# One weight block for both token halves, in two banks by turns, in the gate and z projections of a hybrid decoder layer

## The reference, cut to what matters

```python
hn = rms_norm(x, norm_mix)
proj = einsum('bsd,dn->bsn', hn, w_in) + b_in
z_att = proj[..., OFF_Z_ATT:OFF_GATES]                       # 512 channels
gates = sigmoid(proj[..., OFF_GATES:].reshape(b, s, 2, 1024)) # 2048 channels
...
att = sum(softmax(lse over groups) * out of each group)       # 512 channels
y_att = att * silu(z_att)
merged = gates[:, :, 0] * (y_rnn @ w_o_rnn) + gates[:, :, 1] * (y_att @ w_o_att)
x = x + merged @ w_out
x = x + sigmoid(rms_norm(x) @ w_ple_gate + b) * (p @ w_ple)
```

## Time and profile before

| what | value |
|---|---|
| median of 3 runs | 1347.05 us (1346.85 to 1347.11) |
| the profiled execution, its time | 1346.43 us |
| its span, first to last instruction | 1344.6 us |
| PE busy | 1330.4 us, 99% |
| DVE, ACT, POOL busy | 788.4, 506.8, 535.5 us |

### The profile page before, as it was taken

The page is one execution under the profiler, slowest core; times in us unless marked ns, Lnnn a source line. Parts: engine busy times, 40 slices in busy tenths (PEclk is TensorE's granted clock), DMA queues, the critical chain, the costliest instruction groups (busy, mean ns, idle before and its releaser), DMA issues.

```text
span 1344.6 us, 17628 instructions
## 1 busy us (share of the span) xinstructions
PE 1330.4 (99%) x6254; PEld 1103.4 (82%) x6254; DVE 788.4 (59%) x1257; ACT 506.8 (38%) x1281; POOL 535.5 (40%) x500
## 2 busy tenths in 40 slices
PE   8999999999999999999999999999999999999998
PEld 6887888888888888888888888888888788888887
DVE  6799888842779666565665752159612466234323
ACT  7455646542434444344443688311200011223100
POOL 6975424404458334041340632353166317044020
PEclk9999999999999999999999999999999999999999
DMA  6232312332202032120320332376379545122111
GB/s 239 79 102 87 104 61 79 110 100 71 75 13 83 25 90 66 29 83 24 95 59 29 114 102 85 99 244 211 102 280 414 178 129 154 58 79 63 40 48 47
DMA packets 84470, 139.50 MB, mean 104 GB/s; under 512 B 10048, under 2 KB 41120, under 8 KB 84384
## 3 DMA queue, kind: packets, MB, share of 16 engines
q10 hardware_dynamic: 39936, 75.82, 15.9%
q1 hardware_dynamic: 44448, 62.56, 15.7%
HBM read 108.84 MB, written 29.51 MB: 103 GB/s over the span
## 4 chain that ended last, share of the span: by engine, by line
PE 86%; DVE 5%; DMA 5%; ACT 2%; issue 1%; POOL 0%; SPq 0%; ACTq 0%; POOLq 0%; DVEq 0%
PE bank L1257 26%; PE bank L1262 26%; PE bank L1261 26%; DMA g_in<-gate_dram 4%; PE bank L1407 2%; PE bank L1387 2%; PE bank L1374 1%; PE bank L1396 1%; DVE xc L991 1%; PE bank L1500 1%; DMA x_nat<-in_x 0%; ACT L736 0%; DVE ibuf L1018 0%; PE bank L1300 0%; DVE qkr L1099 0%
## 5 line engine op out<-in xcount | busy, mean ns | idle before, releaser
L539 POOL TENSOR_TENSOR ring<-raw,ring 128x512 fp32r<-128x512 f32 x221 | 311.8, 1411 | 724.7 <-PE bank L1262 642.3
L1257 PE MATMUL bank<-hn,ring 128*128 128x512 f32 x640 | 251.8, 393 | 2.3 <-DVE sgbuf L979 1.2
L1262 PE MATMUL bank<-hn,ring 128*128 128x512 f32 x640 | 249.4, 390 | 0.0
L1261 PE MATMUL bank<-hn,ring 128*128 128x512 f32 x640 | 249.2, 389 | 0.0
L1257 PE MATMUL bank<-ring,hn 128*128 128x512 f32 x576 | 232.6, 404 | 0.2 <-POOL ring L539 0.2
L1262 PE MATMUL bank<-ring,hn 128*128 128x512 f32 x576 | 225.8, 392 | 0.0
L1261 PE MATMUL bank<-ring,hn 128*128 128x512 f32 x576 | 225.2, 391 | 0.0
L543 POOL TENSOR_SCALAR ring<-raw 128x512 fp32r<-128x512 f32 x221 | 186.6, 844 | 8.2 <-DMA raw<-in_w_rnn_s 8.1
L1257 PEld LDWEIGHTS bank<-hn,ring 128*128 128x128 f32 x640 | 120.2, 188 | 27.4 <-DVE sgbuf L979 1.6
L1262 PEld LDWEIGHTS bank<-hn,ring 128*128 128x128 f32 x640 | 120.1, 188 | 25.4
L1261 PEld LDWEIGHTS bank<-hn,ring 128*128 128x128 f32 x640 | 120.2, 188 | 23.9
(11 more groups left out here) (181 smaller groups left out, 2157.4 us busy)
## 6 DMA issues: line engine op xcount, KB each, us to landing
raw<-in_w_tail_s SPq DMA_DIRECT2D x104, 256.0 KB, 2.7
g_in<-gate_dram ACTq DMA_DIRECT2D x48, 256.0 KB, 3.1
raw<-in_w_rnn_s SPq DMA_DIRECT2D x45, 256.0 KB, 2.7
raw<-in_w_qkv_s SPq DMA_DIRECT2D x48, 192.0 KB, 2.5
gate_dram<-g_out ACTq DMA_DIRECT2D x32, 256.0 KB, 2.1
raw<-in_w_qkv_s SPq DMA_DIRECT2D x48, 128.0 KB, 2.2
o_dram<-o_buf ACTq DMA_DIRECT2D x48, 128.0 KB, 1.8
o_in<-o_dram ACTq DMA_DIRECT2D x12, 512.0 KB, 3.7
```

The lines of the kernel that those rows point to most:

```text
L539: nc.gpsimd.tensor_tensor(ring[:, ring_slot(p), 1], raw[:, p % RAW], ring[:, ring_slot(p), 0].bitcast(F32), ALU.subtract).then_inc(w_ready, 1)
L1257: ins = T.matmul(out, lhs[0], rhs[0], start=first, stop=False)
L1261: T.matmul(out, lhs[0], rhs[1], start=False, stop=False)
L1262: return T.matmul(out, lhs[1], rhs[0], start=False, stop=last)
```

## The change

Slots 2m and 2m + 1 are taken together as a pair. For each block of weights TensorE runs six matmuls: high by high for half 0 and half 1, high by low for both, low by high for both. So successive products alternate between two banks, and both banks are complete at the end of the pair. TensorE waits for both banks at the pair's start. The order list puts both slots of a pair at the pair's end; attention steps stay after the same number of products.

```diff
-        if K % KD == 0:
-            order.append(("slot", K // KD - 1))
+        slot = K // KD - 1
+        if K % KD == 0 and slot < SLOTS_Q:
+            order.append(("slot", slot))
+        elif K % (2 * KD) == 0 and slot >= SLOTS_Q:
+            order += [("slot", slot - 1), ("slot", slot)]
         if K in STEP_AT:
             order.append(("step", STEP_AT[K]))
...
+            def both_halves(n, first_block, blocks, rhs_of, after_block):
+
+                for b in range(blocks):
+                    p, c = divmod(first_block + b, 4)
+                    need(p)
+                    w_hi, w_lo = part(p, slice(c * P, (c + 1) * P))
+                    x_hi, x_lo = zip(*(rhs_of(h)(b) for h in range(2)))
+                    for i, (w, x) in enumerate(((w_hi, x_hi), (w_hi, x_lo), (w_lo, x_hi))):
+                        for h in range(2):
+                            ins = T.matmul(bank[(n + h) % 4][:], w, x[h], start=b == 0 and i == 0,
+                                           stop=b == blocks - 1 and i == 2)
+                            if used[0]:
+                                ins.then_inc(w_used, used[0])
+                                used[0] = 0
+                            if b == blocks - 1 and i == 2:
+                                ins.then_inc(proj_done, 1)
+                    if c == 3:
+                        used[0] = 1
+                    after_block(b)
 
             for q, (kind, t, h) in enumerate(Z_MAIN):
                 n = N_Z + q
                 bank_free(n)
-                transposed(n, 4 * FIRST_TAIL + (q // 2) * KD, KD, perm_half(h), h == 1, step_after(q))
+                if h == 0:
+                    bank_free(n + 1)
+
+                    def steps_after(b):
+                        for K in (KD * (SLOTS_Q + q) + 2 * b + 1, KD * (SLOTS_Q + q) + 2 * b + 2):
+                            if K in STEP_AT:
+                                attention(STEP_AT[K])
+
+                    both_halves(n, 4 * FIRST_TAIL + (q // 2) * KD, KD, perm_half, steps_after)
```

## The result

| | before | with the change |
|---|---|---|
| median of 5 runs on one chip | 1347.11 us (1346.85 to 1348.13) | 1352.93 us (1350.76 to 1353.99) |
| the profiled execution: time, span | 1346.43, 1344.6 us | 1350.76, 1348.9 us |

The ratio is 1.0041, 95% interval 1.003 to 1.0052: slower by 5.8 us. The profiled execution with the change is the fastest of its five, so it shows less than the median has; the others are taken up in the experiments.

The account below looks back on a forecast made before the run. TensorE was taken as the bound, busy throughout 846 to 983 us at full clock. Waits of 1.4 + 2.8 + 0.2 + 1.4 = 5.8 us on 1347.05 gave 1352.85, stated as 1352.8, range 1349.9 to 1356.3 us.

Parts of the forecast that it names:

- slot 26: Where TensorE would wait some 2.8 us for z banks that DVE reads late; bounds 0.5 and 4.5 us.
- No gain from alternation: All 960 gate and z products: changing banks leaves their distance as it was, so no change in time.
- The rival of 0.216: Alternation shortens the products' distance to the bf16 warm-up's: minus 10.3 us, net 1346.0 us with sharper waits; chance 0.07.
- Two sigmoids in a row: ACT at pair ends: work behind comes 1.40 us later; TensorE waits 0.79 us at K = 672, 0.59 at 624.
- Statistics a slot late: Row DMAs behind slot 16's sigmoid start 5.21 us later, delaying the merges; waits 2.8 us at slot 26, 0.2 at 30.
- nothing catches up: The chain from the statistics' DMAs through the merges keeps its whole 5.21 us delay; rival that it recovers, chance 0.13.
- are read in time: Banks of gate slots cause no wait; the tightest, slot 19, has its sigmoid end about 0.3 us before its deadline.
- The last gates: Slot 39's sigmoid and DMA come 1.40 us later, lengthening TensorE's `g_in` wait by that; bounds 0.5 and 2.0.
- a late start isn't made up: Behind slot 39, DMA is at its limit, so the gate loads keep the 1.40 us delay.
- The clock: Rival: TensorE's clock falls, by bank cycling or a 2.8 us standstill; ten half-speed products cost 2 us, 1354.9; chance 0.05.
- it stood at most 1.5 so far: Within the clock rival: TensorE's longest standstill in the kernel before was 1.5 us, against 2.8 us with the change.
- The rule of the same page of the Trainium skill on cycling through banks: Cycling PSUM banks makes TensorE's clock fall back, 1.2 GHz for part of the stage; kept as a rival within 0.05.

Follow-up runs that it names:

- e10: The changed kernel run a third time, all slots 0 to 39 in pairs, for another profile: 1352.95 us against 1347.31 before.
- e1: The changed kernel run again, all slots in pairs, for a second profile: median 1353.45 us, ratio 1.0051; its profiled execution took 1357.47 us.
- e7: The changed kernel with the edits of e5, e6 and e8 together: 1345.64 us, ratio 0.9989 to the kernel before.
- e9: The kernel before with 120 products on zeros added behind the warm-up, in five rows by type, bank and accumulation: bf16 0.2154 us, fp32 0.2267 us each.
- e2: The changed kernel with only slots 0 to 15 in pairs, the others one by one as before: 1348.04 us, ratio 1.0012.
- e8: The changed kernel with the attention step put ahead of the pair's two slots on ACT and DVE at K = 624 and 672: 1351.11 us, ratio 1.0029.
- e5: The changed kernel with the DMAs of the statistics' rows issued at the head of slot 16, not behind its sigmoid: 1351.64 us, ratio 1.003.
- e4: The changed kernel with only slots 36 to 39 in pairs, the others one by one as before: 1349.42 us, ratio 1.0017.
- e3: The changed kernel with only slots 16 to 35 in pairs, the others one by one as before: 1349.61 us, ratio 1.0022.
- e6: The kernel before with four loads of x moved from the head of the second O stage to the third: 1345.94 us, ratio 0.9989.

## Why the prediction was right, and where its sizes were off

The forecast was 1352.8, in the range 1349.9 to 1356.3, slower with 0.82; measured were 1352.93 and, on another chip, 1353.45 against 1346.55. PE runs the same number of matmuls up to each place in both kernels, so the start of each can be set beside the start of the same one before. What PE lost at each place, in us, in the three profiles of the change:

| place | forecast | first (1350.76) | e10 (1352.95) | e1 (1357.47) |
|---|---|---|---|---|
| before the first pair | 0 | 0.5 | -0.1 | 2.5 |
| the steps behind K = 624 and 672 | 1.4 | 1.3 | 1.3 | 1.3 |
| slot 22 | 0 | 0.3 | 0.3 | 0.4 |
| slot 26 | 2.8 | 0.7 | 2.7 | 2.5 |
| the clock behind slot 26 | 0 | 0 | 0 | 1.6 |
| slot 30 | 0.2 | 0 | 0 | 0 |
| `g_in`, beyond before, with the clock behind it | 1.4 | 1.4 | 2.2 | 2.7 |
| sum | 5.8 | 4.2 | 6.4 | 11.0 |

The terms one by one:

- *No gain from alternation.* Right. The view that told it was three neighbouring distances, and a bank change among them; e7 and e9 confirm it. The rival of 0.216 is out: that distance belongs to bf16.
- *Two sigmoids in a row, 1.4 us.* Right. The waits are 0.4 + 0.65 = 1.1, and PE loses 1.3; 1.5 by e2's median. I had taken 0.31 us from the exponential's end to PE; it was 0.30 at K = 630, and the exponential there ended 0.2 earlier against PE's deadline than I had worked out. e8 shows that the order of the list is the cause.
- *Statistics a slot late, 2.8 us, and 0.2 at slot 30.* The mechanism is right (5.2 us at the rows' DMAs; e5 takes it away). Its size varies with how DVE and POOL meet: 0.5, 2.2 and 2.4 us in three executions of the change. My "nothing catches up" was wrong in the first of them and held in the other two. No wait at slot 30 was seen in any profile. At slot 22, for which I had put nothing because the banks of gate slots "are read in time", PE waited 0.2 us for slot 19's bank, the one that I had called tightest, and lost 0.3.
- *The last gates, 1.4 us.* The delay is right (1.4 at slot 39's sigmoid), the wait varies: 2.8, 2.6 and 2.1 us against 1.5, and 3.0 in e4. So "a late start isn't made up" held in some executions and not in e10; where the last gates come as before, the wait varies too (1.0 in e2, 1.8 in e3). By time the part costs 2.9. The sum had no term for what a longer wait does to the clock, which is 1.6 of the 2.2 and 2.7 in e10 and e1; for e4 no profile shows it.
- *The clock.* I gave it 0.05 as a rival of its own. Behind the waits it is a surcharge: after waits on `g_in` of 2.1, 2.3, 2.4 and 2.6 us (e10, e8, e5, e1) eight products ran at 1.2 GHz, 1.6 us more; after 2.8 and 3.0 (the first profile of the change, e4) they did not, and after 1.5 (before), 1.0 (e2) and 1.8 us (e3) neither. In e5 the fall came five products behind the wait. At slot 26 the clock fell behind the wait of 2.2 us in e1, and not behind that of 2.4 in e10. Pairs aren't needed for it: between 10 and 20 us the granted clock was 0.83, 0.67 and 0.83 in e1, e2 and e3, in e2 with no wait over 1.4 us ahead of it. And "it stood at most 1.5 so far" had overlooked a wait of 1.9 us at the start of the kernel before, which no fall followed. The Trainium skill says why a wait can do that: its page "TensorE: Matmul & The Clock Gate", section "What's actually happening", has the throttled state as the default, which activity releases. The traces agree as far as the two levels and the idling before them go; that the longest wait escaped shows that length alone doesn't decide it. The rule of the same page of the Trainium skill on cycling through banks, which I had weighed, did not show: over the 960 products by turns, 749 to 985 us, the granted clock stayed at 1.00 in the first profile and in e7.

That my sum met the median is partly luck: the clock was missing, and the wait at slot 26 comes out at a quarter of its term or near the whole of it, so that the same kernel takes 1350.76 us or 1352.95. What stays open: how often the clock falls, and where. The mean granted clock is below 1.00 in 11 of the 12 executions of the change (the first five, e1 and e10) and in 28 of 52 of the kernel before beside e1 to e8, but also in 10 of 11 of e2, which has no long wait; it doesn't say where the clock fell. Open is also what e4 costs beyond its wait, and what makes the rest of the difference between e10's and the first profile's merges.

## What to carry to other kernels

Before regrouping work on the bound engine, look at the distance between its instructions where what you mean to vary already varies; if the distance is the same there, the regrouping can only move waits. Taking two outputs together delays the first by a whole slot and makes both due at once: go through everything that stands behind it in the readers' queues, above all a chain of small DMAs whose slack was a few microseconds. A wait of two or three microseconds on TensorE can cost more than itself, because the clock may fall behind it.

## What the runs showed that I had not expected

- TensorE's products of 128 x 128 by 512 columns start 0.2154 us apart in bf16 and 0.2267 in fp32 as used here, whether they add up or start anew, in one bank or in two by turns (e9, on zeros, and behind the first nine of the fp32 products started anew; in the kernel 0.2267 on data).
- A DVE operation of 2.2 us took 3.1 and a POOL operation of 1.3 us took 3.2 where the two met in time; which of them was longer differed between executions of the same program.
- The loads of x, 2 MB in front of one gate load, cost the kernel before its wait of 1.5 us on `g_in`: moved behind the second O stage, they give 1.2 us back (e6, ratio 0.9989).
